# Expert stage of a two-block transformer step: inputs copied out of all assignments in expert order, nine weight slots, x summed in place, the last w2 slabs in halves

## The chip, the core and the metric

The kernel runs on one core of one Trainium2 chip. The metric is the device time of one launch in microseconds (us). The kernel is written engine by engine, with explicit semaphores: TensorE (PE) for matrix products and transposes, VectorE (DVE), ScalarE (ACT), GpSimd (POOL) and SyncE (SP). SP issues nearly all weight loads on one DMA queue; POOL issues small ones.

## The reference, cut to what matters

256 tokens of width 1024 go through a first block (attention, MLP, a state-space mixer, MLP) and a second one of two layers. Each layer of the second block is a token mixer and then a mixture of experts. Only the experts matter here:

```python
def hier_moe(h, ...):                      # h: 256 x 1024, float32
    eid, wts = ...                         # per token: top-1 group, top-2 experts of its 8; 32 experts in all
    order = argsort(eid)                   # 512 assignments (256 tokens x 2) in expert order
    for each block of assignments of one expert e:
        xb = h[tok_b]
        hid = silu(xb @ w1[e]) * (xb @ w3[e])      # w1, w3: 1024 x 512
        out[tok_b] += (hid @ w2[e]) * w_b          # w2: 512 x 1024
x = x + gate2 * out
```

Every expert's weights are read once per layer: 32 x 3 slabs of 2 MB, 96 slabs or 201 MB per layer.

## The kernel before, in words

The stages run one after the other: in, attn, mlp0, ssm, mlp1, mix0, moe0, mix1, moe1, end. `mix_*` and `moe_*` are the programs of one engine for a layer `l` (`moe_pe`, `moe_act`, `moe_dve`, `moe_pool`, `moe_sp`). Each engine waits on the semaphores of the events that it needs (`at(...)`), and each engine's program is a fixed order written out by hand.

**Pairs.** The expert stage works through `NP` = 16 pairs of experts. Each expert has room for `CAP` = 64 tokens, so a pair fills 128 columns. A flag sends the whole layer to a general path (`general_*`) when an expert has more than 64 tokens. For pair i PE does, in this order:

- `inner(i, "exp_w1")`: 16 products of 64 columns of weights against 512 columns, two experts side by side in the array; the same for `"exp_w3"`. The input is `xg`, the pair's tokens turned to columns.
- `combine(i - 1)`: four products of 128 x 512 that spread the pair before back over the 256 tokens.
- `turn_h(i)`: four transposes of the hidden rows. It waits for DVE's product `x_h`.
- `gather(i + 1)`: 16 products of 128 x 128 of the rows `H2` with a 0/1 matrix `psel` picks the next pair's tokens. ACT then scales them into `xg` (`turned_x`).
- `turn_w(i + 1)`: two transposes of the routing weights.
- `outer(i)`: 16 products with w2. It waits for ACT's copy of the turned hidden rows.

DVE makes `psel` (`places`), the weighted matrix (`weigh`), the product, the gate (`rows_out`) and the sums into `av` (`combine`).

**Weight slots.** `Places` hands out slots of 2 MB in turn. `load` takes the next slot, waits until its last tenant is free (`("free", key)`, given by PE when it has read the slab) and issues the DMA. SP does this strictly in program order: w1, w3, w2 of both experts of pair 0, then pair 1 and so on. I number the slabs 0 to 95: slabs 6i to 6i+5 belong to pair i. In the expert stage eight slots turn: four of the ring, two in the arena (`("extra", l)`, free when the mixer's branch products have been read), XTGB (free after the router) and `slot7` at the arena's end (also after `("extra", l)`). Slab n waits for slab n-8 to be read. The two slabs of the mixer's `out_w` take ring slots just before.

**Ahead of and behind the stage.** In `mix_sp` the last loads are three `branch_w` slabs and two `out_w` slabs. `moe_pool` loads the next layer's gate rows (`gate_rows`, 512 KB) and `gate_b` at the stage's start, or the final gain in layer 1. After the last pair of layer 0 a norm of x is formed, its transpose is made, and mix1 starts. After layer 1 the final norm is stored.

Of the kernel before, what the change touches and what calls it, by code (L numbers as in the profile page):

```python
# [12 lines left out]
P = 128  # L13
T = 256
# [163 lines left out]
def build(nc, d, out, consts):  # L178
    with ExitStack() as ctx:
# [15 lines left out]
        LATE = ("cm", "dmask", "rope2c", "rope2s")  # L195
        for name, width in consts.items():
            if name not in LATE:
                C[name] = sb("c_" + name, [P, width])[:, :]
        ASZ = 27124
        arena = Arena(sb("arena", [P, ASZ])[:, :], ASZ)  # L200
        posi = sb("posi", [P, 2], I32)[:, :]
        flag = sb("flag", [P, 2], I32)[:, :]
        modc = [sb(f"modc{l}", [P, 512])[:, :] for l in range(2)]
# [3 lines left out]
        for name in ("x0", "x1", "aq0", "aq1", "aq2", "aq3", "ident", "rope", "consts", "c", "pos", "gb", "sink", "ssmp", "late", "ada_b", "cols", "mod", "gate_b",  # L207
                     "fox_fb", "mla_g", "abias", "router_b", "rw", "srow", "se0", "se1", "se2", "out"):
            sems[name] = ctx.enter_context(nc.semaphore("s_" + name))
        for i in range(NRING + 4):  # L210
# [13 lines left out]
        ring = Places(slots + [None, None, XTGB, None])  # L224
# [10 lines left out]
        def slab(sp, key, name, off, kc, n, hold=False):  # L235
            load(sp, key, d[name][off:off + P * kc * n].rearrange("(p f) -> p f", p=P), kc, n, hold)

# [184 lines left out]
        def in_pool(pool):  # L422
# [3 lines left out]
            for name in consts:  # L426
                if name not in ("half", "ones", "ident", "ropec", "ropes") + LATE:
# [3 lines left out]
            pool.then_inc(pool.e.memset(C["ones"], 1.0), "ones")  # L431
# [444 lines left out]
        h00 = arena.get(2, 512)  # L876

# [16 lines left out]
        def gate_rows(pool, l, i, *events):  # L894

            pool.wait_ge(at("mod", l), *events)
            pool.landed(pool.e.dma_start(MOD[:, i, :], bcast(dmod[l][2 * i:2 * i + 2, :].rearrange("a n -> (a n)")
# [59 lines left out]
        s_E = [arena.get(2, 768) for _ in range(3)]  # L957
        spare = C["maska"]
# [69 lines left out]
        def ssm_pe(pe):  # L1028
# [10 lines left out]
            def sums():  # L1039

                pe.wait_ge(at("a"), at("consts"), at("ones"))
# [58 lines left out]
            def norm_b(g):  # L1100
                ps = bank(pe, "sn", g)
                pe.wait_ge(at("ysq", g), at("ones"))
# [222 lines left out]
        arena.pos = 0  # L1325
        for name in LATE:
            C[name] = arena.get(consts[name])
        ctab, stab = C["rope2c"], C["rope2s"]
        posf = small[:, 40:42]
        MOD = arena.get(6, D)  # L1330
# [9 lines left out]
        h01 = arena.get(2, 512)  # L1340
        rs2 = small[:, 60:62]
# [41 lines left out]

        def mlp1_pool(pool):
            pool.stage("mlp1")
            pool.wait_ge(at("XT", 3, 1))
            for name in ("cm", "dmask"):
                pool.landed(pool.e.dma_start(C[name], d["const_" + name]), "late", "late")
# [120 lines left out]
        H2, av = MOD[:, 0:2, :], MOD[:, 3:5, :]  # L1509
# [11 lines left out]
        def mix_sp(sp, l):  # L1521
# [46 lines left out]
        def causal_act(act, l, br, h, what, bufs):  # L1568
# [16 lines left out]
            elif h % 2 == 0:  # L1585
                act.wait_ge(at("cv", *k, h))
                act.then_inc(act.cp(yT[br][:, h, :], ps_of("cv", *k, h)[:, 0:T]), ("yT", l, br), ("read", "cv", *k, h))

        def causal_dve(v, l, br, h, what, bufs):
# [22 lines left out]
            elif h % 2 == 1:  # L1612
                v.wait_ge(at("cv", *k_, h))
                v.then_inc(v.cp(yT[br][:, h, :], ps_of("cv", *k_, h)[:, 0:T]), ("yT", l, br), ("read", "cv", *k_, h))
# [274 lines left out]
        def mix_dve(v, l, nn):  # L1889
# [26 lines left out]
            v.wait_ge(at("late"))  # L1916
# [40 lines left out]
            v.wait_ge(lfk, at("ones"))  # L1957
# [97 lines left out]
            for t in range(2):  # L2055
                for n in range(2):
# [3 lines left out]
                    k = v.then_inc(v.tt(o, ps_of("ob", l, t, n), MOD[:, 2, n * 512:(n + 1) * 512], ALU.mult),  # L2060
                                   ("read", "ob", l, t, n))
                    v.wait_ge(k)
                    v.then_inc(v.tt(X[:, t, hs], (av if l else X)[:, t, hs], o, ALU.add), ("rows", nn + 1, t),
# [40 lines left out]
        slot7 = arena.ap[:, ASZ - SLAB:]  # L2104
        assert arena.pos <= ASZ - SLAB
# [8 lines left out]
        g_y = slots[3][:, 0:2 * D].rearrange("p (t f) -> p t f", t=2)  # L2114
# [688 lines left out]
```

## Time and profile before

| what | value |
|---|---|
| runs | 2397.36, 2399.67, 2400.62 us (median 2399.67) |
| profiled execution | 2398.69 us |
| its span, first to last instruction | 2396.8 us |
| PE busy | 2354.6 us, 98% |
| DVE, ACT, POOL busy | 36%, 18%, 3% |
| mean granted TensorE clock | 0.994 |
| chain that ended last | PE 96%, DVE 2%, DMA 1% |
| HBM traffic | 666.56 MB read, mean 279 GB/s |

The span is the hardware profiler's; the device time is 1.9 us longer. The page's 40 slices show a DMA rate of 427 to 428 GB/s in the slices of both expert stages and 90 to 310 GB/s nearly everywhere else. "Busy" of PE counts from an instruction's start to a modelled end, so that it overlaps; for durations the distance between starts or the pieces of the chain serve better.

### The profile page before, as it was taken

Reading aid. Unit: us, or ns where it says so; the run is one execution under the profiler, and the core shown is the slowest. Engines: PE = TensorE matmul, PEld = TensorE weight load, DVE = VectorE, ACT = ScalarE, POOL = GpSimd, SP = SyncE. Lnnn points to the kernel's source line nnn. Section 1 sums busy time; section 2 is a strip of 40 time slices with the busy share of each in tenths; the row PEclk is TensorE's granted clock in tenths of the full one; section 3 lists DMA queues with packets and bytes.
Section 4 is the critical chain, followed back from the end, with each engine's and each line's share of the span. In section 5 each row is a group of like instructions: output and inputs, shape, how many; then the busy total and the mean of one; then the engine's idle time right before and its main releaser. Section 6 shows DMA issues by size and latency. Waiting matters only on the chain.

```text
span 2396.8 us, 24315 instructions
## 1 busy us (share of the span) xinstructions
PE 2354.6 (98%) x10366; PEld 1398.3 (58%) x10366; DVE 873.2 (36%) x1711; ACT 426.8 (18%) x967; POOL 74.3 (3%) x129
## 2 busy tenths in 40 slices
PE   8999999999999999999899999999999999999998
PEld 5578447875586448787444444444878644444443
DVE  3455326667355334463212222122355322112112
ACT  3310003256110011220111111101122011111111
POOL 2000000010100000000000000000000000000000
PEclk9999999999999999999999999999999999999999
DMA  7367645354577743244899999994324599999996
GB/s 281 130 229 294 276 185 195 139 192 160 189 291 271 308 147 144 96 171 181 344 428 427 427 428 428 427 427 158 114 92 170 220 373 427 428 428 427 428 428 265
DMA packets 53241, 669.44 MB, mean 279 GB/s; under 512 B 7216, under 2 KB 7504, under 8 KB 13824
## 3 DMA queue, kind: packets, MB, share of 16 engines
q1 hardware_dynamic: 46512, 649.45, 66.8%
q0 software_dynamic: 6608, 18.30, 2.3%
q8 instruction: 86, 1.41, 0.2%
q14 instruction: 35, 0.29, 0.0%
HBM read 666.56 MB, written 1.16 MB: 279 GB/s over the span
## 4 chain that ended last, share of the span: by engine, by line
PE 96%; DVE 2%; DMA 1%; issue 0%; ACT 0%; POOL 0%; SPq 0%; DVEq 0%; POOLq 0%; ACTq 0%
PE ps L101 93%; DVE arena L117 1%; PE ps L298 1%; DMA arena<-ssm_rows 1%; PE ps L2294 1%; DVE arena L114 0%; PE ps L569 0%; PE ps L2276 0%; DMA X<-in_x 0%; PE ps L1559 0%; DVE arena L110 0%; PE ps L1036 0%; POOL small L117 0%; ACT arena L106 0%; DVE arena L122 0%
## 5 line engine op out<-in xcount | busy, mean ns | idle before, releaser
L101 PE MATMUL ps<-ring,arena 128*64 128x512 f32 (+1 forms) x2368 | 703.2, 594 | 0.0
L101 PE MATMUL ps<-arena 128*128 128x128 f32 (+7 forms) x3088 | 671.5, 438 | 5.6 <-DVE arena L117 3.7
L101 PE MATMUL ps<-XTGB,ring 128*128 128x256 f32 x2800 | 618.6, 380 | 0.0
L101 PEld LDWEIGHTS ps<-XTGB,ring 128*128 128x128 f32 x2800 | 527.6, 190 | 78.7 <-issue 5.9
L101 PEld LDWEIGHTS ps<-ring,arena 128*64 128x64 f32 (+1 forms) x2368 | 264.2, 156 | 401.0 <-issue 400.1
L101 PEld LDWEIGHTS ps<-arena 128*128 128x128 f32 (+2 forms) x3088 | 337.5, 167 | 206.6 <-issue 188.9
L117 DVE TENSOR_TENSOR arena<-arena,ps 128x512 f32<-128x512 f32 x152 | 104.4, 687 | 412.3 <-PE ps L101 412.3
L101 PE MATMUL ps<-ring,XTGB 128*128 128x512 f32 (+3 forms) x568 | 226.8, 557 | 0.6 <-ACT XTGB L105 0.6
L117 DVE TENSOR_TENSOR arena<-ps,arena 128x512 f32<-128x512 f32 (+3 forms) x144 | 86.3, 634 | 318.9 <-PE ps L101 318.6
L101 PEld LDWEIGHTS ps<-ring,XTGB 128*128 128x128 f32 x568 | 106.1, 192 | 113.4 <-issue 108.0
L101 PE MATMUL ps<-XTGB,arena 128*64 128x512 f32 x384 | 169.1, 593 | 1.4 <-ACT arena L121 1.4
L121 ACT COPY arena<-ps 128x512 f32<-128x512 f32 (+2 forms) x166 | 74.1, 467 | 505.1 <-PE ps L2294 327.6
L105 ACT ACTIVATE arena<-ps 128x512 f32<-128x512 f32 x80 | 47.2, 597 | 651.7 <-PE ps L101 651.7
L117 DVE TENSOR_TENSOR arena<-arena 128x256 f32<-128x256 f32 (+8 forms) x220 | 109.1, 508 | 113.4 <-ACT arena L105 108.8
L114 DVE SCALAR_TENSOR_TENSOR arena<-ring,small,arena 128x512 f32<-128x512 f32 x168 | 126.3, 752 | 6.0
L122 DVE COPY arena<-ps 128x256 f32<-128x256 f32 (+3 forms) x64 | 29.7, 469 | 240.3 <-PE ps L2276 118.0
L101 PEld LDWEIGHTS ps<-XTGB,arena 128*64 128x64 f32 x384 | 51.9, 137 | 107.2 <-issue 105.4
L105 ACT ACTIVATE arena<-ps,small 128x128 f32<-128x128 f32 (+1 forms) x264 | 100.0, 457 | 66.9 <-PE ps L101 66.8
L114 DVE SCALAR_TENSOR_TENSOR arena<-arena 128x256 f32<-128x256 f32 (+1 forms) x212 | 87.8, 438 | 52.2 <-ACT arena L105 29.1
L128 DVE RECIPROCAL arena<-arena 128x2 f32<-128x2 f32 (+2 forms) x84 | 90.0, 1071 | 3.8 <-ACT arena L106 1.8
L101 PE MATMUL ps<-arena,ring 128*128 128x256 f32 x384 | 83.2, 379 | 0.0
L101 PEld LDWEIGHTS ps<-arena,ring 128*128 128x128 f32 x384 | 72.8, 190 | 9.8
(155 smaller groups left out, 781.6 us busy)
## 6 DMA issues: line engine op xcount, KB each, us to landing
ring<-in_exp_w SPq DMA_DIRECT2D x96, 2048.0 KB, 18.8
arena<-in_exp_w SPq DMA_DIRECT2D x72, 2048.0 KB, 20.1
ring<-in_mlp_w SPq DMA_DIRECT2D x32, 2048.0 KB, 7.8
ring<-in_ada_w SPq DMA_DIRECT2D x24, 2048.0 KB, 8.2
XTGB<-in_exp_w SPq DMA_DIRECT2D x24, 2048.0 KB, 17.3
ring<-in_ssm_w_in SPq DMA_DIRECT2D x12, 2048.0 KB, 7.8
ring<-in_w_in SPq DMA_DIRECT2D x12, 2048.0 KB, 7.9
ring<-in_gate_w SPq DMA_DIRECT2D x12, 2048.0 KB, 7.9
```

Source lines behind the costliest of these rows:

```text
L101: return self.e.matmul(o, lhsT=lhsT, rhs=rhs, start=start, stop=stop, skip_group_check=True)
L105: return self.e.activation(o, i, func, bias=bias, scale=scale)
L114: return self.e.scalar_tensor_tensor(out=o, in0=i0, scalar=s, in1=i1, op0=op0, op1=op1)
L117: return self.e.tensor_tensor(o, a, b, op)
L121: return self.e.copy(o, i)
L122: return self.e.tensor_copy(o, i)
L128: return self.e.reciprocal(o, i)
L298: ins = pe.e.transpose(ps[:, j * P:(j + 1) * P], i, C["ident"][0:m, 0:m])
L2294: ins = pe.e.transpose(ps[:, f * P:(f + 1) * P], x_h[:, f:512:4], C["ident"])
```

## The change

- **Order.** `order()` on DVE, run in pair 0, forms the start of each expert in the list of all 512 assignments by five doubling sums (`cnt`), writes the starts as integers (`wsi`, at most `LAST` = 448), corrects `code` for late experts, and builds `selc`, a 256 x 512 matrix of 0 and 1 that puts each assignment into its place.
- **Compaction.** PE's `compact(c)` multiplies each of the eight chunks of `H2` by `selc`: two products of 128 x 512 per chunk. Four chunks go behind `combine(0)` in pair 1, four behind `combine(1)` in pair 2. ACT scales them into `compA` and `compB`. `compA` lies over the tables `cm` and `dmask`, which are loaded again at the end of layer 0 (`late_tables`).
- **From the fourth pair on** (`ND` = 3) PE's `gather` is left out. ACT's `window(i)` reads two starts into registers and copies four blocks of 4 x 64 columns out of the compacted rows.
- **Order on PE.** `combine` is cut in halves: one ahead of `turn_h`, one behind it. In pair 0 the halves of `gather(1)` stand there.
- **Nine slots.** Two slots at the arena's end, 7 and 8, are free when the mixer's attention is done; the two `out_w` slabs take them. Slab n then waits for slab n-9.
- **x in place.** The experts' sums go into `X`. A copy of `X` (1 MB) is written to DRAM at the stage's start, for the general path. Gate rows and final gain are loaded after the last compaction.
- **Last w2.** In pair 15 the two w2 slabs are loaded as four half slabs (first output half of both, then the second half).
- `ones` becomes a view of `tri`; `maska`, `ropec`, `ropes` and `modc` move into the arena.

```diff
+        def slabs_in_halves(sp, keys, name, offs, kc, n):
+            place = {}
+            for h in range(2):
+                for j, (key, off) in enumerate(zip(keys, offs)):
+                    if h == 0:
+                        place[key], was = ring.take(key)
+                        if was is not None:
+                            sp.wait_ge(at("free", was))
...
+                    sp.landed(sp.e.dma_start(o, src), f"half{j}" if h else f"ring{place[key]}", ("w half" if h else "w", key))
# mix_sp
+            for j in (4, 3):
+                ring.tenant[NRING + j] = ("attention", l)
+            ring.turn[0:0] = [NRING + 4, NRING + 3]
# moe_pool
-            pool.wait_ge(at("rows", nn - 1, 1))
+            pool.wait_ge(at("rows", nn - 1, 0), at("rows", nn - 1, 1))
+            pool.landed(pool.e.dma_start(dkeep[l], X), "keep", ("keep", l))
+            pool.landed(pool.e.dma_start(iota, d["const_iota512"]), "iota", ("iota", l))
             if l == 0:
-                gate_rows(pool, 1, 2)
                 pool.landed(pool.e.dma_start(gb, d["gate_b"][P:2 * P, :]), "gate_b", ("gate_b", 1))
+                gate_rows(pool, 1, 2, at("comp", l, 7))
+                pool.wait_ge(at("xg ready", l, NP - 1, 0), at("xg ready", l, NP - 1, 4))
+                late_tables(pool, 1)
# moe_pe
+            def compact(c):
+                ps = bank(pe, "comp", l, c)
+                pe.wait_ge(at("selc", l))
+                for t in range(2):
+                    ins = pe.mm(ps, H2[:, t, c * P:(c + 1) * P], selc[:, t, :], t == 0, t == 1)
+                pe.then_inc(ins, ("comp", l, c))
...
                 inner(i, "exp_w3")
                 if i >= 1:
-                    combine(i - 1)
+                    combine(i - 1, 0)
+                else:
+                    gather(1, 0)
                 turn_h(i)
+                if i >= 1:
+                    combine(i - 1, 1)
+                else:
+                    gather(1, 4)
+                for c in COMPACT.get(i, ()):          # {1: (0, 1, 2, 3), 2: (4, 6, 5, 7)}
+                    compact(c)
+                if 1 <= i < ND - 1:
+                    gather(i + 1, 0)
+                    gather(i + 1, 4)
                 if i + 1 < NP:
-                    gather(i + 1)
                     turn_w(i + 1)
                 outer(i)
# moe_act
+            def window(i):
+                act.wait_ge(at("comp ready", l), at("starts", l), at("exp_w3", l, i - 1))
+                first = [start_of(act, 2 * i + j) for j in range(2)]
+                for c0, comp in ((0, compA), (4, compB)):
+                    for j in range(2):
+                        act.then_inc(act.cp(xg[:, c0:c0 + 4, 64 * j:64 * j + 64], comp[:, :, bass.ds(first[j], CAP)]),
+                                     ("xg ready", l, i, c0))
```

## Rows read from the trace of the kernel before

**Rows 1.** The page: busy time, share and instructions of each engine.
```profile
PE 2354.6 (98%) x10366; PEld 1398.3 (58%) x10366; DVE 873.2 (36%) x1711; ACT 426.8 (18%) x967; POOL 74.3 (3%) x129
```

**Rows 2.** Windows: stretch, length, busy by engine, clock, DMA share, GB/s.
```profile
1560.00:1590.00 30.00, 30.00 (x150) 13.04 (x148) 5.25 (x9) 4.19 (x10) 0.00 (x0) 1.00 1.01 428
```

**Rows 3.** The chain in moe0: start, length, what; one pair.
```profile
1206.68 3.57 PE ps L101 x32
...
1210.47 24.38 PE ps L101 x104
...
1239.11 24.38 PE ps L101 x104
```

**Rows 4.** Tile view, time to landing of the last slab, issued at 1575.35.
```profile
DMA to landing us min/median/max: 31.7/31.7/31.7
```

**Rows 5.** The chain around the last pair of moe0.
```profile
1607.21 0.48 PE ps L2294 x4
...
1608.40 9.87 PE ps L101 x38
```

**Rows 6.** Timeline of SP: the issues of weight slabs (x2: two slabs).
```profile
1149.84 0.33 SPq L233 DMA_DIRECT2D XTGB<-in_exp_w  x1
...
1169.08 0.80 SPq L233 DMA_DIRECT2D ring<-in_exp_w  x2
...
1188.88 0.81 SPq L233 DMA_DIRECT2D ring<-in_exp_w  x2
...
1202.62 0.80 SPq L233 DMA_DIRECT2D ring<-in_exp_w  x2
1217.53 0.80 SPq L233 DMA_DIRECT2D arena<-in_exp_w  x2
...
1246.17 0.92 SPq L233 DMA_DIRECT2D ring<-in_exp_w  x2
```

**Rows 7.** Tile view, time to landing of slab 8, issued at 1169.08.
```profile
DMA to landing us min/median/max: 7.8/7.8/7.8
```

**Rows 8.** Tile view, time to landing of slab 12, issued at 1188.88.
```profile
DMA to landing us min/median/max: 9.4/9.4/9.4
```

**Rows 9.** Tile view, time to landing of slab 17, issued at 1202.99.
```profile
DMA to landing us min/median/max: 19.8/19.8/19.8
```

**Rows 10.** Timeline of PE in pair 0 of moe0: `turn_h(0)`.
```profile
1177.28 0.75 PE L2294 MATMUL ps<-c_ident,arena 128*128 128x128 f32 x4 [0.86 <-DVE arena L117]
```

**Rows 11.** Timeline of PE: `combine(14)`, four products of 128 x 512 (two passes each).
```profile
1603.51 3.70 PE L101 MATMUL ps<-arena 128*128 128x512 f32 x8
```

**Rows 12.** DMA view: issues, KB each, median us to landing.
```profile
arena<-mod POOLq DMA_DIRECT2D x4, 512.0 KB, 12.5
...
arena<-in_const_dmask POOLq DMA_DIRECT2D x1, 768.0 KB, 11.1
...
arena<-in_const_cm POOLq DMA_DIRECT2D x1, 192.0 KB, 6.1
```

**Rows 13.** Tile view, time to landing of slab 93 in moe0, issued at 1568.49.
```profile
DMA to landing us min/median/max: 27.5/27.5/27.5
```

**Rows 14.** Tile view, time to landing of slab 93 in moe1, issued at 2336.39.
```profile
DMA to landing us min/median/max: 27.7/27.7/27.7
```

**Rows 15.** The chain at the last `outer` of moe1.
```profile
2376.31 9.87 PE ps L101 x38
```

**Rows 16.** Windows: an idle stretch of PE, the stretch behind, and a short gap.
```profile
1618.70:1622.60 3.90, 0.42 (x1) 0.00 (x0) 1.92 (x4) 2.71 (x4) 0.56 (x1) 1.00 0.93 384
...
1624.20:1627.80 3.60, 3.48 (x4) 1.45 (x5) 2.38 (x6) 0.68 (x2) 2.05 (x2) 0.53 0.08 32
...
573.00:576.00 3.00, 2.33 (x20) 1.38 (x19) 2.90 (x7) 0.19 (x1) 0.63 (x1) 1.00 0.00 0
```

**Rows 17.** Timeline of ACT in moe0, last pair.
```profile
1607.72 0.58 ACT L121 COPY arena<-ps 128x512 f32<-128x512 f32 x1 [10.36 <-PE ps L2294]
```

**Rows 18.** Source view: ACT loads a register.
```profile
L2209 ACTq TENSOR_LOAD <-flag x1: 479/479/479, 1210.3 to 1210.3; - x1
```

More of the change, by code:

```diff
@@ L220, in build @@
                 sems[f"gen{l}_w{j}"] = ctx.enter_context(nc.semaphore(f"s_gen{l}_w{j}"))
-        ring = Places(slots + [None, None, XTGB, None])
+            sems[f"gen{l}_x"] = ctx.enter_context(nc.semaphore(f"s_gen{l}_x"))
+        ring = Places(slots + [None, None, XTGB, arena.ap[:, ASZ - 2 * SLAB:ASZ - SLAB], arena.ap[:, ASZ - SLAB:]])
         ring.begin(NRING)
@@ L1382, in mlp1_sp, with late_tables @@
             mlp_sp(sp, 1)
+        def late_tables(pool, l):
+            for name in ("cm", "dmask"):
+                pool.landed(pool.e.dma_start(C[name], d["const_" + name]), "late", ("late", l))
         def mlp1_pool(pool):
@@ L1386, in mlp1_pool @@
             pool.wait_ge(at("XT", 3, 1))
-            for name in ("cm", "dmask"):
-                pool.landed(pool.e.dma_start(C[name], d["const_" + name]), "late", "late")
+            late_tables(pool, 0)
             for i in (2, 5):
@@ L1586, in causal_act @@
                 act.wait_ge(at("cv", *k, h))
-                act.then_inc(act.cp(yT[br][:, h, :], ps_of("cv", *k, h)[:, 0:T]), ("yT", l, br), ("read", "cv", *k, h))
+                act.then_inc(act.cp(yT[br][:, h, :], ps_of("cv", *k, h)[:, 0:T]), ("yT", l, br), ("read", "cv", *k, h),
+                                *([("free", ("attention", l))] if br == 2 else []))
         def causal_dve(v, l, br, h, what, bufs):
@@ L1613, in causal_dve @@
                 v.wait_ge(at("cv", *k_, h))
-                v.then_inc(v.cp(yT[br][:, h, :], ps_of("cv", *k_, h)[:, 0:T]), ("yT", l, br), ("read", "cv", *k_, h))
+                v.then_inc(v.cp(yT[br][:, h, :], ps_of("cv", *k_, h)[:, 0:T]), ("yT", l, br), ("read", "cv", *k_, h),
+                              *([("free", ("attention", l))] if br == 2 else []))
         def mix_pe(pe, l, nn):
@@ L2113, in build @@
         g_u = x_h.rearrange("p (a b) -> p a b", a=2)
-        g_y = slots[3][:, 0:2 * D].rearrange("p (t f) -> p t f", t=2)
+        g_y, g_x = [slots[3][:, 2 * D * i:2 * D * (i + 1)].rearrange("p (t f) -> p t f", t=2) for i in range(2)]
+        g_a = arena.ap[:, xbase:xbase + 2 * D].rearrange("p (t f) -> p t f", t=2)
+        dkeep = [nc.dram_tensor(f"x{l}", (T, D), F32).ap().rearrange("(t p) f -> p t f", t=2) for l in range(2)]
         g_h = xg.rearrange("p a b -> p (a b)").rearrange("p (a b) -> p a b", a=4)
@@ L2235, in moe_sp @@
                         slab(sp, (nm, l, i, j), nm, (l * NE + 2 * i + j) * P * SLAB, 8, 512)
-                for j in range(2):
-                    slab(sp, ("exp_w2", l, i, j), "exp_w2", (l * NE + 2 * i + j) * P * SLAB, 4, 1024)
+                keys = [("exp_w2", l, i, j) for j in range(2)]
+                offs = [(l * NE + 2 * i + j) * P * SLAB for j in range(2)]
+                if i < NP - 1:
+                    for key, off in zip(keys, offs):
+                        slab(sp, key, "exp_w2", off, 4, 1024)
+                else:
+                    slabs_in_halves(sp, keys, "exp_w2", offs, 4, 1024)
             general(sp, l, reg, general_sp)
@@ L2317, in outer, with combine @@
                         pe.then_inc(ins, ("xy", l, i, n), *([("free", ("exp_w2", l, i, j)) for j in range(2)] if n else []))
[L2319 to L2328 removed]
+            def combine(i, n):
+                pe.wait_ge(at("pwt ready", l, i), at("xy ready", l, i, n))
+                for t in range(2):
+                    ps = bank(pe, "xc", l, i, t, n)
+                    pe.then_inc(pe.mm(ps, pwt[i % 2][:, t * P:(t + 1) * P], x_y[:, n * 512:(n + 1) * 512],
+                                      True, True), ("xc", l, i, t, n))
+            for c0 in (0, 4):
+                gather(0, c0)
             for t in range(2):
@@ L2378, in moe_act @@
                              ("xht ready", l, i), ("read", "xht", l, i))
-                if i + 1 < NP:
+                for c in COMPACT.get(i, ()):
+                    compact(c)
+                if i + 1 < ND:
                     turned_x(i + 1)
+                elif i + 1 < NP:
+                    window(i + 1)
                 if i == 1:
@@ L2529, in moe_dve @@
                     weigh(i + 2)
+                if i == 0:
+                    order()
             rows_out(NP - 1)
@@ L2669, in constants @@
     c["ident"] = np.eye(P, dtype=f)
-    c["ones"] = None
     c["half"] = None
```

188 lines of the change are left out of this document (125 added, 63 removed).

## Prediction, made before the change was run

> **What bounds the kernel now.** I read the page first. PE is busy 98% of the span [rows 1], so a change that takes matrix products away looks like a gain. The windows show that this is only half of it: in the expert stages the DMA engines are full as well, 428 GB/s with a share of 1.01 [rows 2]. So I compare the two by pair. On the chain of moe0 the starts of the same piece lie 1239.11 - 1210.47 = 28.64 us apart [rows 3]; that is PE's time for a pair. The six slabs of a pair cost the DMA: slab 8 lands at 1169.08 + 7.8 = 1176.9, slab 12 at 1188.88 + 9.4 = 1198.3, slab 17 at 1202.99 + 19.8 = 1222.8 [rows 6 to 9]. The last five take 24.5 us, 4.90 each, which agrees with 2.097 MB at 428 GB/s; six take 29.4 us. **DMA is therefore slower than PE by 0.7 us a pair**, and PE hides it only with the lead that it gets from slabs loaded during the mixer. At the end that lead is gone: the last slab lands at 1575.35 + 31.7 = 1607.05 [rows 4], and the `outer` that reads it starts at 1608.40 [rows 5]. Taking work off PE can't shorten a stage whose transfers end 1.3 us before they are needed. Only an earlier or fuller DMA queue can, or a shorter chain behind the last slabs.
>
> When does the queue stand idle? Slab 8 is issued at 1169.08 when `inner(0, "exp_w1")` frees its slot, after slab 7 has long landed. Between slabs 8 and 12 lie 21.4 us, 1.9 more than four transfers: slab 12 was issued at 1188.88, when `outer(0)` freed its slot, and the queue ran dry at 1176.9 + 3 x 4.9 = 1191.6 (slab 11), only 2.7 us later. From issue to first byte it takes 7.8 - 4.9 = 2.9 us with an empty queue, and 9.4 - 4.9 = 4.5 us here [rows 7, 8]. Slab 18, issued at 1217.53 [rows 6], was 5.3 us ahead of slab 17's landing and lost nothing, by the full windows behind it.
>
> **The change part by part.** Everything is counted in moe0; moe1 repeats it.
>
> *PE's units.* A piece of 24.38 us holds 48 products that run two by two and 4 full ones, 28 units of 0.87 us [rows 3]; the four of `combine` alone read 3.70 us [rows 11], so 0.87 to 0.93. An `inner` or `outer` is 8 units, 6.97 us, half a `combine` 1.74.
>
> *Gathers gone.* 3.57 us each [rows 3], 13 of 16: -46.4 us of PE a layer. *Compaction:* eight chunks of two full products, 16 x 0.87 = +13.9 us, 6.97 in each of pairs 1 and 2. From pair 3 on a pair takes 28.64 - 3.57 = 25.07 us. Net -32.5 us of PE, nearly all of it worth nothing, because the DMA's 29.4 us a pair are then late.
>
> *Ninth slot.* Nine slabs instead of eight are in before PE frees the first slot at 1169.08: the slab for the slot behind the mixer's first `out_w` (about 1137), its second, and the one into XTGB at 1149.84 [rows 6]. The DMA is idle before 1169.08, so the ninth is free: **-4.9 us** on everything behind.
>
> *Pair 0.* PE waits 0.86 us for DVE ahead of `turn_h(0)` [rows 10]; half a gather now covers that. `outer(0)` frees its slots 0.86 us earlier, 3.5 us before the queue is dry: idle at most 1.0 instead of 1.9. **-0.9 us**.
>
> *Pair 1, a new idle.* Slab 19 (slab 18 takes the place that slab 17 had, and lands at 1222.8 - 0.9 = 1221.9) needs slab 10's slot, freed by `outer(1)`. That end moves from 1217.53 to 1217.53 - 0.86 + 6.97 = 1223.6, with the queue already empty. First byte at +2.9 = 1226.5: **+4.6 us**.
>
> *Pair 2, again.* Slab 24 ends at 1226.5 + 6 x 4.9 = 1255.9. Slab 25 needs `outer(2)`, at 1246.17 - 0.86 + 13.94 - 3.57 = 1255.7 [rows 3, 6]. First byte 2.9 to 4.5 us later, 1258.6 to 1260.2: **+2.7 to +4.3 us**. The gate rows of 512 KB (1.2 us at 428 GB/s) [rows 12], now issued after the last compaction, fall into this gap and cost nothing more. From pair 3 on PE frees slots 4.3 us a pair faster than they fill, so no further idle.
>
> Sum for the DMA: -4.9 - 0.9 + 4.6 + (2.7 to 4.3) = **+1.5 to +3.1 us**: the four edits that should feed the queue are more than eaten by the compaction, which holds back two releases at the worst moment.
>
> *Reloaded tables,* moe0 only: 768 + 192 KB [rows 12] issued when `xg` of pair 15 is ready, into a full queue ahead of slab 93: 0.98 MB / 428 GB/s = **+2.3 us**. I count them fully, since windows at 1.01 leave no room beside them; below, 0. The copy of X (1 MB), the 512-wide counts and `gate_b` run in the idle stretch that ends at 1169.08: some 3 us beside one slab issued at 1149.84, 0 (if late, at most 2).
>
> *Behind the last slabs.* PE catches the DMA up: slab 19 lands at 1231.4 and pair 3 starts near 1256, a lead of 24.5 us that shrinks by 4.3 a pair, so from pair 9 on PE waits for w1 and w3 of every pair. In the last pair slab 93 decides. Before it lands at 1568.49 + 27.5 = 1596.0 [rows 13] and `outer(15)` starts 12.4 us later. After: 0.2 for the semaphore, `inner` 6.97, half a combine 1.74 (covers DVE's product), `turn_h` 0.48 [rows 5], the other half 1.74 (covers ACT's copy of 0.58 [rows 17]) = 11.1 us. The w2 slabs need 9.8 us, so they are in; **halves gain nothing** (if their smaller rows slowed them by up to a third, the second half would still come before 11.1 + 3.5 us).
>
> moe0: 1596.0 + (1.5 to 3.1) + 2.3 + 11.1 = 1610.9 to 1612.5 against 1608.40 [rows 5]: **+2.5 to +4.1 us**. moe1: slab 93 lands at 2336.39 + 27.7 = 2364.1 [rows 14]; + (1.5 to 3.1) + 11.1 = 2376.7 to 2378.3 against 2376.31 [rows 15]: **+0.4 to +2.0 us**. Behind `outer(15)` both orders are the same.
>
> *Clock.* New idle gaps of PE appear from pair 9 on: 2.7 us ahead of w3 (9.8 - 6.97) and about 1.5 ahead of w1. The rows show the granted clock at 0.53, the level of 1.2 GHz, for 3.6 us behind an idle stretch of nearly 3.9 us, and still 1.00 where PE was busy 2.33 of 3.00 us [rows 16]. My gaps lie between the two. A fall costs half of 3.6, 1.7 us, and inside the stage the waits absorb it; it counts only in the last `inner` or `outer`: 0 to 1.7 us a layer. I take 0.6 each, 1.2 in all.
>
> On such gaps the Trainium skill ("TensorE: Matmul & The Clock Gate", section "HAM oscillation") is blunter: it describes a kernel whose bursts are shorter than its waits for weights and which is throttled anew at each of them. By that rule every wait here would be paid with slow products; the trace of before, whose expert stages have no such gaps, can't confirm it. It is the third rival.
>
> *ACT, DVE, POOL, SP.* ACT's window is two register loads of 0.48 [rows 18] and four copies of 256 elements, at most 0.58 each [rows 17], 3.3 us after the x_ht copy; PE passes 1.74 + 0.22 + 6.97 us before it needs them. Queued behind it on ACT is only the next silu. `order()` adds some twenty DVE instructions in pair 0, where DVE is busy 5.9 of 30 us in such a window [rows 2]; only `rows_out(0)` stands behind, 14 us ahead of its reader. POOL waits with nothing behind it but the flag and the norm. SP is held up by the attention's end for the two `out_w` slabs, which are needed tens of us later. All 0; if the register loads drained ACT, up to 5 us a pair would still be covered.
>
> **Sum.** 2.5 to 4.1 + 0.4 to 2.0 = +2.9 to +6.1, middle 4.5, with the clock 5.7. The profiled execution took 2398.69 us (span 2396.8 and 1.9 around it), 1.0 below the median of 2399.67: 2398.7 + 5.7 = 2404.4, or 2405.4 from the median. **I predict 2405 us.**
>
> **Rivals.**
>
> 1. *The queue is never dry (faster).* The place is slabs 19 and 25. If `outer(1)` and `outer(2)` freed their slots 4.5 us before the queue ends, the -5.8 us would stand: moe0 1596.0 - 5.8 + 2.3 + 11.1 = 1603.6 (-4.8), moe1 2364.1 - 5.8 + 11.1 = 2369.4 (-6.9): 2387. It decides once PE's compaction costs under about 1.5 us a pair, or the lead is larger than I count. Against it: 0.87 us a product is read off. 12%.
> 2. *No change.* The idle at slab 25 vanishes because PE is a little faster than counted and slab 24 slower; that takes 2.7 to 4.3 off each layer: -2 us in all, 2397. 20%.
> 3. *The clock (slower still).* All three waits of a pair, from pair 9 on, end in a fall: 25.07 + 3 x 1.7 = 30.2 us, 0.8 above the DMA's 29.4, over seven pairs and two layers 11 us: 2398.7 + 4.5 + 11 = 2415. 11%.
> 4. *The windows are late.* PE waits for ACT in each of 13 pairs; 1 us beyond the covered stretch would cost 13 a layer less the slack of 4.3 a pair. 5%, near 2410.
>
> **How the numbers follow.** My forecast (2401 to 2409 with its clock) has 52%. Within 0.2%, 4.8 us, is about what a measurement can't tell from no change. Of the forecast 60% lies above +4.8: 0.31, with rivals 3 and 4 0.47 slower. Same: 0.21 and most of rival 2, 0.36. Faster: rival 1 and a rest of 2, 0.17. The range leaves out rival 1's core and the far end of 3: 2391 to 2413.
>
> **What would show it.** Landing times: slab 18 near 1222, slab 19 near 1231.4, slab 25 near 1264 (1261.9 before); SP's issue of slabs 19 and 25 with an empty queue; windows below 400 GB/s near 1224 and 1257; PE's chain in the last pairs waiting on the DMA with 29.4 us a pair; slab 93 of moe0 near 1601, of moe1 near 2366; PE's busy share down by some 60 us and a clock below 0.99. If PE shows no wait on weights in the late pairs, or slab 25 lands before 1259, I am wrong.

## The result, and the profile after

The changed kernel takes **2404.97 us** (median of 9 runs, 2403.39 to 2408.97) against 2399.67 us before; the ratio is 1.0026 with a 95% interval of [1.0015, 1.0036]. It is slower by some 5 us, and whether by more than 0.2% the interval leaves open. The profiled execution took 2406.85 us, 1.9 above its own median, while that of before lay 1.0 below its own; the two traces therefore differ by 8.2 us and the medians by 5.3. The section on the prediction says which terms this touches.

The page of the changed kernel, busy time and then the chain of waits by engine:

```profile
PE 2313.4 (96%) x9598; PEld 1329.6 (55%) x9598; DVE 881.3 (37%) x1751; ACT 395.2 (16%) x879; POOL 77.6 (3%) x134
...
PE 83%; DMA 14%; DVE 2%; issue 0%; ACT 0%; POOL 0%; SPq 0%; DVEq 0%; POOLq 0%; ACTq 0%
```

PE does 41 us less than before [rows 1], and the kernel is longer all the same: 14% of the chain is now DMA. The time is lost in the stretches that the windows of the changed kernel show (stretch, length, busy by engine, clock, DMA share, GB/s): two in pairs 1 and 2, and three around the last `inner` of moe0:

```profile
1222.50:1227.50 5.00, 5.00 (x26) 1.63 (x24) 1.29 (x2) 0.00 (x0) 0.00 (x0) 1.00 0.32 69
1257.50:1261.50 4.00, 4.00 (x20) 1.28 (x18) 0.81 (x2) 0.00 (x0) 0.00 (x0) 1.00 0.87 310
1600.00:1602.60 2.60, 0.44 (x3) 0.00 (x0) 0.00 (x0) 0.60 (x1) 0.00 (x0) 1.00 0.97 370
1602.80:1606.40 3.60, 3.60 (x10) 1.34 (x12) 0.00 (x0) 0.00 (x0) 0.00 (x0) 0.53 1.04 385
1606.50:1610.00 3.50, 3.50 (x18) 1.38 (x16) 0.00 (x0) 0.00 (x0) 0.00 (x0) 1.00 1.05 386
```

Near 1224 the queue moves 69 GB/s while PE is fully busy: PE is still at the compaction and holds the slot that the next slab needs. Before, the expert stages run at 428 GB/s [rows 2]. The landing times of the slabs that were issued into these gaps, from the tile view (slab 19, issued at 1225.1; slab 25, at 1257.1; slab 93 of moe0, at 1568.3; slab 93 of moe1, at 2342.2; each line is one slab's time from issue to landing):

```profile
DMA to landing us min/median/max: 8.1/8.1/8.1
...
DMA to landing us min/median/max: 9.2/9.2/9.2
...
DMA to landing us min/median/max: 34.3/34.3/34.3
...
DMA to landing us min/median/max: 30.6/30.6/30.6
```

So slab 19 lands at 1233.2, slab 25 at 1266.3, and slab 93 at 1602.6 and 2372.8. A slab that took 8.1 us had an empty queue in front of it, as slab 8 had before [rows 7]. The chain of the changed kernel in moe0 (start, length, what) reads first as before, then differently:

```profile
1218.03 22.66 PE ps L101 x100
...
1249.96 22.66 PE ps L101 x100
...
1275.03 22.66 PE ps L101 x100
...
1300.11 22.66 PE ps L101 x100
...
1364.18 29.31 DMA arena<-in_exp_w
...
1393.63 10.70 PE ps L101 x36
...
1568.32 34.27 DMA ring<-in_exp_w
1602.59 0.14 issue
1602.73 10.70 PE ps L101 x36
1613.42 0.47 PE ps L2370 x4
1613.89 11.52 PE ps L101 x42
```

Without its gather a pair takes PE 1300.11 - 1275.03 = 25.08 us (before 28.64 [rows 3]). From pair 3 on PE is therefore faster than the DMA, catches it up near 1380 and then waits. The end of the stage is the landing of slab 93 plus what stands behind it; the last `outer` starts at 1613.89 + 1.72 = 1615.6 against 1608.40 [rows 5].

To compare stages I take POOL's instruction in the normalisation that ends each of them. Timeline of POOL in the changed kernel, behind moe0, behind the mixer and behind moe1 (start, length, what, idle before):

```profile
1627.59 0.56 POOL L117 TENSOR_TENSOR small<-small,c_half 128x1 f32<-128x1 f32 x1 [43.55 <-DVE small L111]
...
1923.20 0.56 POOL L117 TENSOR_TENSOR small<-small,c_half 128x1 f32<-128x1 f32 x1 [16.14 <-DVE small L111]
...
2396.10 0.56 POOL L117 TENSOR_TENSOR small<-small,c_half 128x1 f32<-128x1 f32 x1 [373.10 <-DVE small L111]
```

The same instruction stands at 1149.86 ahead of moe0. Before, the four are 1148.97, 1620.44, 1916.81 and 2388.36. As stage lengths in us, with the experiments of the next section:

```
                       moe0    mixer   moe1
before                471.5    296.4   471.6
changed               477.7    295.6   472.9
e1_double             491.5    298.5   486.9
e2_narrow             472.7    296.1   468.8
e3_eight              480.6    295.8   478.9
e5_tables_later       477.1    296.0   475.0
e6_whole_w2           474.8    297.9   474.2
e7_filler             475.9    296.1   473.3
e4_no_copying         470.4    296.2   469.4
e8_no_copying_whole   470.1    295.6   469.6
e9_no_copying_eight   469.5    296.8   470.3
e10_no_copying_uncut  472.1    296.6   471.7
```

One execution stands in each line. e6 differs from the changed kernel only where nothing waits (below), so its 2.9 us less in moe0 and 1.3 more in moe1 are roughly what one stage varies by. The changed kernel's moe0 is 6.3 us longer than before in these traces; e5, e6 and e7, which do nearly the same work, are 5.6, 3.3 and 4.4 longer, so 6.3 is the high end.

### The profile page after: what moved, and what is told of

Its sections match the earlier page's. It is cut to its first block, busy times and chain, and to the rows that moved or that the text cites. A ratio compares the mean times of both kernels' runs of the same rounds, so it can differ in the third digit from the quotient of the medians.

```text
span 2405.0 us, 23014 instructions
## 1 busy us (share of the span) xinstructions
PE 2313.4 (96%) x9598; PEld 1329.6 (55%) x9598; DVE 881.3 (37%) x1751; ACT 395.2 (16%) x879; POOL 77.6 (3%) x134
## 4 chain that ended last, share of the span: by engine, by line
PE 83%; DMA 14%; DVE 2%; issue 0%; ACT 0%; POOL 0%; SPq 0%; DVEq 0%; POOLq 0%; ACTq 0%
PE ps L101 81%; DMA ring<-in_exp_w 8%; DMA arena<-in_exp_w 5%; DVE arena L117 1%; PE ps L322 1%; DMA arena<-ssm_rows 1%; DVE arena L114 0%; PE ps L2370 0%; DMA ring<-in_attn_w_in 0%; PE ps L592 0%; PE ps L1600 0%; PE ps L2352 0%; PE ps L1061 0%; DVE arena L110 0%; ACT arena L106 0%
## 5 line engine op out<-in xcount | busy, mean ns | idle before, releaser
L101 PE MATMUL ps<-arena 128*64 128x512 f32 (+7 forms) x2640 | 697.1, 517 | 23.3 <-DMA arena<-in_exp_w 17.7
L101 PEld LDWEIGHTS ps<-arena 128*64 128x64 f32 (+2 forms) x2640 | 290.2, 160 | 333.6 <-issue 309.9
L117 DVE TENSOR_TENSOR arena<-ps,arena 128x512 f32<-128x512 f32 (+4 forms) x166 | 96.0, 613 | 358.1 <-PE ps L101 345.1
L117 DVE TENSOR_TENSOR arena<-arena,ps 128x512 f32<-128x512 f32 x32 | 22.0, 688 | 463.8 <-PE ps L101 463.8
L101 PE MATMUL ps<-XTGB,arena 128*64 128x512 f32 x320 | 148.9, 620 | 12.0 <-DMA ring<-in_exp_w 11.9
L121 ACT COPY arena<-ps 128x512 f32<-128x512 f32 (+3 forms) x167 | 74.6, 467 | 518.2 <-PE ps L2370 338.9
L105 ACT ACTIVATE arena<-ps 128x512 f32<-128x512 f32 (+1 forms) x81 | 47.6, 594 | 677.9 <-PE ps L101 677.8
L114 DVE SCALAR_TENSOR_TENSOR arena<-arena 128x256 f32<-128x256 f32 (+2 forms) x216 | 90.8, 444 | 51.1 <-ACT arena L105 28.6
L117 DVE TENSOR_TENSOR X<-X,ps 128x512 f32<-128x512 f32 x128 | 88.1, 688 | 40.0 <-PE ps L101 40.0
L122 DVE COPY arena<-ps 128x256 f32<-128x256 f32 (+5 forms) x67 | 30.2, 455 | 183.3 <-PE ps L101 121.3
```

Of the source, the lines that this page charges most:

```text
L101: return self.e.matmul(o, lhsT=lhsT, rhs=rhs, start=start, stop=stop, skip_group_check=True)
L105: return self.e.activation(o, i, func, bias=bias, scale=scale)
L114: return self.e.scalar_tensor_tensor(out=o, in0=i0, scalar=s, in1=i1, op0=op0, op1=op1)
L117: return self.e.tensor_tensor(o, a, b, op)
L121: return self.e.copy(o, i)
L122: return self.e.tensor_copy(o, i)
```

## The experiments

My theory was that the compaction in pairs 1 and 2 holds back two slot releases, that the DMA queue runs dry there, and that every microsecond of this reaches the end because the stage is bound by transfers. The rivals: the waits of PE in the late pairs (its clock), the reloaded tables, the windows on ACT, and that the gain of the gathers was only hidden by something small at the end. e1 to e3 price the theory, e4 takes its cause away, e5 to e7 test the rivals, and e8 to e10 ask what in the change is worth keeping.

**e1_double: the compaction at twice its price.**

```diff
-                for t in range(2):
+                for t in (0, 1, 0, 1):
                     ins = pe.mm(ps, H2[:, t, c * P:(c + 1) * P], selc[:, t, :], t == 0, t == 1)
```

> The changed kernel with each compaction product run twice, the second pass over the first, so that the values stay the same; PE gets 16 more products of 0.87 us a layer, 6.9 us in each of pairs 1 and 2. My theory: in these pairs PE decides when slots come free, so the DMA stands idle for just that time: slab 19 starts 6.9 us later, slab 25 another 6.9 us minus what it now overlaps, some 12 us a layer, 25 in all: 2430 us. Rival (PE has slack in a stage that waits for weights, compaction is free): 2405. Rival (the clock and the additional small transfers made the loss): 2405 too.

2436.74 us (5 runs, 2436.39 to 2436.83), ratio 1.0156 [1.0142, 1.0170]: 31.8 us above the changed kernel. Windows of e1 where slabs 19 and 25 are due, and POOL's instruction behind moe0 and moe1:

```profile
1222.00:1234.00 12.00, 12.00 (x66) 5.33 (x67) 2.47 (x5) 3.02 (x8) 0.00 (x0) 1.00 0.15 38
1258.00:1272.00 14.00, 14.00 (x56) 5.16 (x56) 2.47 (x5) 2.78 (x6) 0.54 (x1) 1.00 0.50 184
```

```profile
1640.72 0.56 POOL L117 TENSOR_TENSOR small<-small,c_half 128x1 f32<-128x1 f32 x1 [41.54 <-DVE small L111]
...
2426.07 0.56 POOL L117 TENSOR_TENSOR small<-small,c_half 128x1 f32<-128x1 f32 x1 [373.17 <-DVE small L111]
```

The queue stands idle for 11.3 us ahead of slab 19 and 8.4 ahead of slab 25, where the changed kernel had 5.1 and 2.9. The stages grow by 13.8 and 14.0 us, and the added products are 13.9 us a layer: **close to one for one**. Counted from POOL's instruction ahead of the stage, slab 25 lands 12.1 us later than in the changed kernel in moe0 and 13.3 in moe1, about the 12 that I had expected; the rest comes behind it and is within what a stage varies by. The mixer adds 2.9, all of it between POOL's first and second instruction behind moe0 (7.9 against 4.9 us); I can't explain it. All of this work was given to the engine that waits for weights from pair 7 on: that it costs nearly its full length shows that the bound isn't PE's total but when PE frees slots.

**e2_narrow: the compaction at a quarter of the columns.**

```diff
-                    ins = pe.mm(ps, H2[:, t, c * P:(c + 1) * P], selc[:, t, :], t == 0, t == 1)
+                    ins = pe.mm(ps[:, 0:P], H2[:, t, c * P:(c + 1) * P], selc[:, t, 0:P], t == 0, t == 1)
```

> The changed kernel with each compaction product 128 columns wide instead of 512; the copied inputs of the assignments beyond the first 128 are wrong. PE loses 10.4 us of work a layer in pairs 1 and 2, nothing else changes: nine slots, all transfers, the copies, the late gaps stay. My theory: the idle stretch of the DMA ahead of slab 19 shrinks from 4.6 to about 1 us and the one ahead of slab 25 vanishes, 6 us a layer, 12 in all: 2393 us, below the kernel before. Rival (compaction is hidden, the loss lies in the clock, the small transfers or the half slabs): 2405, no change.

2396.58 us (11 runs), ratio 0.9989 [0.9980, 0.9998]: 8.4 us below the changed kernel. Windows of e2 at the same places:

```profile
1222.00:1227.00 5.00, 5.00 (x26) 1.68 (x24) 0.00 (x0) 0.60 (x1) 0.00 (x0) 1.00 1.00 419
1257.00:1260.00 3.00, 3.00 (x13) 0.95 (x10) 0.69 (x1) 0.00 (x0) 0.00 (x0) 1.00 1.01 431
```

The gaps are gone (0.8 us ahead of slab 19, none ahead of slab 25), slab 93 of moe0 lands at 1595.7. Of the 6 us a layer that I expected 5.0 and 4.1 came. The timeline of PE shows where the rest of moe0 went:

```profile
1595.82 9.62 PE L101 MATMUL ps<-ring,arena 128*64 128x512 f32 x32 [4.29 <-DMA ring<-in_exp_w]
```

PE was further ahead, waited 4.29 us and ran the last `inner` in 9.62 instead of 7 us. Even with a nearly free compaction this kernel is only 2.4 us faster than before, and e4 below, which saves no gather at all, is as fast or faster (2394.97), while e2 still reloads the tables (2.4 us, see e5). So the gathers saved, 46 us of PE a layer, show no gain of their own.

**e3_eight: the change with eight slots.**

```diff
-            for j in (4, 3):
+            for j in (3,):
-ring.turn[0:0] = [NRING + 4, NRING + 3]
+ring.turn[0:0] = [NRING + 3]
```

> The changed kernel with eight weight slots: the ninth, slot 8, is left out and the second out_w slab goes into a ring slot again. My theory: one transfer of 4.9 us a layer moves behind PE's first release and the dry stretches grow by about 1 us: 6 us a layer, 12 in all: 2417 us. Rival (the slot count doesn't matter once PE waits for weights): 2405. Rival (the ninth slot costs, by an earlier collision in the mixer): below 2405.

2417.70 us (5 runs, 2414.94 to 2419.49), ratio 1.0080 [1.0066, 1.0093]. By the medians the ninth slot is worth 12.7 us here, 6.4 a layer. By the landing of slab 93, counted from POOL's instruction ahead of each stage, it is 4.6 us in moe0 and 4.5 in moe1, close to the 4.9 of one transfer; what the rest of the 12.7 is, I can't say from one trace each (the profiled execution of e3 was the fastest of its five). The window of e3 in pair 1 shows the same gap, one slab earlier in number (it is slab 18 now that waits 5.0 us):

```profile
1217.00:1228.00 11.00, 11.00 (x54) 3.66 (x52) 2.02 (x4) 0.84 (x3) 0.00 (x0) 1.00 0.61 225
```

**e4_no_copying: every pair gathers again,** the rest of the change stays (nine slots, x summed in place, halves, the cut `combine`).

```diff
-        ND = 3
+        ND = NE // 2
-COMPACT = {1: (0, 1, 2, 3), 2: (4, 6, 5, 7)}
+COMPACT = {}
```

(and `order()`, the wide counts, the reloaded tables and the waits for `comp` go, so that the gate rows and the final gain are loaded at the stage's start again.)

> The changed kernel without its copied inputs: every pair's tokens are gathered by PE as before, and order(), the compaction, the 512-wide counts, the windows and the reload of the tables are gone; nine slots, the cut combine, x in place and the half slabs stay. My theory: PE again needs 28.6 us a pair and decides the end, the DMA is 5.8 us a layer ahead of it; what is left of the change is 0.86 us in pair 0 and about 0.9 behind the last slab: 1 to 2.5 us a layer faster than the kernel before, 2395 to 2398. Rival (the copying is what helps and another part costs): above 2405. Rival (nine slots alone bring their 4.9 us a layer): 2388.

2394.97 us (11 runs), ratio 0.9986 [0.9977, 0.9995]: **10.0 us faster than the changed kernel, although PE does 41 us more.** Slab 93 lands at 1590.8 and 2356.4, counted from POOL's instruction ahead of the stage 4.4 and 5.7 us earlier than before, and PE no longer waits for weights. This is what the other edits give together; the copying took it and more.

**e5_tables_later: the reload of the tables behind the last pair.**

```diff
-                pool.wait_ge(at("xg ready", l, NP - 1, 0), at("xg ready", l, NP - 1, 4))
+                pool.wait_ge(at("xy", l, NP - 1, 1))
                 late_tables(pool, 1)
```

> The changed kernel with the reload of cm and dmask at the end of moe0 issued when outer(15) has run, behind all weight slabs, instead of when the input of pair 15 is ready. My theory: 0.98 MB leave the full queue ahead of slab 93, which lands 2.3 us earlier in moe0; moe1 has no reload: 2402.7 us, ratio to before 1.0015. Rival (the small transfers share the engines without cost): 2405, ratio 1.0025. Rival (the tables are now late for mix1): above 2405.

2404.51 us (11 runs), ratio 1.0023 [1.0014, 1.0032], no difference to the changed kernel. Counted from POOL's instruction ahead of moe0, slab 93 lands 2.5 us earlier (1599.2 - 1149.0 against 1602.6 - 1149.9), about the 2.3 that I had put down, though 1.1 of them are there at slab 25 already, ahead of any reload. The reload itself is read best from slab 87 to slab 93, six transfers: 32.1 us in moe0 of the changed kernel, 29.4 in moe0 of e5 and 29.4 in moe1 of both. It costs the queue 2.7 us; in moe0 of e1, e2, e3, e6 and e7, which all reload, it is 2.4 to 2.6. But the stage is only 0.6 us shorter. First the timeline of POOL in e5, then the chain:

```profile
1619.28 0.54 POOL L1417 DMA_DIRECT2D arena<-in_const_cm  x1 [369.02 <-PE ps L101]
1619.81 0.54 POOL L1417 DMA_DIRECT2D arena<-in_const_dmask  x1
```

```profile
1610.22 11.52 PE ps L101 x42
...
1623.67 0.17 DVE small L111
1623.84 2.27 issue
1626.11 0.57 POOL small L117
```

The two issues went onto POOL right ahead of the normalisation's own POOL instruction, which was ready at 1623.84 and started 2.27 us later (0.07 in the changed kernel). In this trace the move exchanged one cost for another.

**e6_whole_w2: the last w2 slabs whole.**

```diff
-                if i < NP - 1:
+                if True:
                     for key, off in zip(keys, offs):
```

> The changed kernel with the last two w2 slabs whole instead of in halves. My theory: outer(15) starts 11.1 us or more behind slab 93, and the w2 slabs need 9.8 whole and 10.8 in halves, so both are in: 0, 2405 us, at most 1 us less because the next stage's loads stand behind 1 us less of transfers. Rival (the halves let outer(15) start early): whole slabs cost up to 2 us a layer, 2409. Rival (the smaller rows hold the queue back and cost): 2403 or less.

2406.20 us (7 runs), ratio 1.0029 [1.0018, 1.0041]: no difference. With slab 93 at 1600.1 the last slab lands at 1609.9, and `outer` can't start before some 11 us after slab 93. In the changed kernel the last half lands at 1613.4 and `outer` starts at 1615.6, so the halves were not waited for either.

**e7_filler: PE kept busy through its waits** from pair 9 on, by products whose result nobody reads.

```diff
+                if i >= 9:
+                    for _ in range(3 if nm == "exp_w3" else 1):
+                        pe.mm(ps, C["ident"], C["tri"], True, True)
                 pe.wait_ge(at("w", (nm, l, i, 0)), at("w", (nm, l, i, 1)))
```

> The changed kernel with filler products in PE's waits: from pair 9 on one product of 128 x 512 of constants ahead of inner w1 and three ahead of inner w3, into the bank that the inner then overwrites; 3.5 us a pair, less than the 4.3 us of slack. My theory: the granted clock of the span goes from 0.986 back to 0.99 or more and the last inner w3 of moe0 takes 7.1 instead of 8.8 us; that is worth 0 to 1.7 us a layer, for only the last inner counts: 2403 to 2405. Rival (the slow clock is the main loss): 2400 or less. Rival (PE has no slack there): 2410 or more.

2404.81 us (11 runs), ratio 1.0024 [1.0015, 1.0033]: no difference that the interval can tell; the granted clock of the span went from 0.986 to 0.992. The timeline of PE in e7 from the filler ahead of the last `inner` of moe0 to that `inner`, then of the changed kernel at the last two `inner` of moe0 and the last one of moe1:

```profile
1597.98 2.84 PE L101 MATMUL ps<-c_tri,c_ident 128*128 128x512 f32 x6
...
1602.44 7.09 PE L101 MATMUL ps<-ring,arena 128*64 128x512 f32 x32 [1.61 <-DMA ring<-in_exp_w]
```

```profile
1591.66 8.78 PE L101 MATMUL ps<-ring,arena 128*64 128x512 f32 x32 [2.57 <-DMA ring<-in_exp_w]
...
1602.73 8.78 PE L101 MATMUL ps<-ring,arena 128*64 128x512 f32 x32 [2.29 <-DMA ring<-in_exp_w]
...
2372.93 7.09 PE L101 MATMUL ps<-ring,arena 128*64 128x512 f32 x32 [2.67 <-DMA ring<-in_exp_w]
```

The filler saves 1.7 us in that one `inner`, and moe0 is 1.8 shorter; moe1, whose last `inner` ran at full clock anyway, is 0.4 longer. So the clock is here a term of at most one such fall a layer; the stage lengths alone, which vary by more, would not show it.

**e8_no_copying_whole, e9_no_copying_eight, e10_no_copying_uncut: what is left.** e8 is e4 with whole w2 slabs; e9 is e8 with eight slots (the edit of e3); e10 is e8 with `combine` whole in every pair and the first gather whole in pair 0, in the order of the kernel before:

```diff
                 if i >= 1:
                     combine(i - 1, 0)
-                else:
-                    gather(1, 0)
+                    combine(i - 1, 1)
                 turn_h(i)
-                if i >= 1:
-                    combine(i - 1, 1)
-                else:
-                    gather(1, 4)
+                if i == 0:
+                    gather(1, 0)
+                    gather(1, 4)
```

> The version that the first four runs point to: nine slots, cut combine, x in place, every pair gathered, no compaction, windows or reload, and the last w2 slabs whole. My theory: PE decides the end and the last slabs come over 3 us before they are needed, so whole or half makes no difference: 2394 to 2396, 4 us below the kernel before. Rival (the halves carry part of the 4 us): 2397 or more.

> The version without copied inputs and with whole w2 slabs, but with eight weight slots instead of nine. My theory: the DMA's last slabs then land 4.9 us later, about 1596 in moe0, which is just where PE wants them; the ninth slot is worth only what PE had to wait, 0 to 2.5 us a layer: 2395 to 2399, against 2394.7 with nine. Rival (the slot is what made that version faster than the kernel before): 2399 or more, all of the 4 us gone. Rival (slots don't matter when PE decides): 2394.7.

> The same version with nine slots, but combine and the gather of pair 0 whole: all of combine(i-1) ahead of turn_h(i), nothing behind it, as in the kernel before. Nine slots and x in place stay. My theory: the 0.86 us in pair 0 and the 0.7 us ahead of outer(15) come back, 1.6 us a layer: 2397.5 to 2398.5. Rival (the nine slots carry the gain): 2394.7.

e8: 2394.69 us, ratio 0.9983 [0.9974, 0.9992], the fastest version of this study. e9: 2396.64 us, 0.9987 [0.9978, 0.9996]. e10: 2398.84 us, 0.9999 [0.9990, 1.0008] (11 runs each). So nearly the whole gain against before, 4.4 us, goes when `combine` and the first gather are no longer cut around `turn_h` (e10; the two intervals just touch, the medians lie 4.2 us apart), and the ninth slot adds 2 us or nothing (e9, intervals overlap). The cut pays at two places of a layer only. In e10 the two waits of PE that it had filled are back; timeline of PE at `turn_h(0)` and at the last `outer` of moe0:

```profile
1177.87 0.75 PE L2366 MATMUL ps<-c_ident,arena 128*128 128x128 f32 x4 [0.86 <-DVE arena L117]
...
1608.99 1.51 PE L101 MATMUL ps<-arena 128*64 128x512 f32 x6 [0.72 <-ACT arena L121]
```

Slab 24 is issued 1.2 us later in moe0 than in e8 and 1.4 in moe1, counted from POOL's instruction ahead of the stage; up to slab 92 nothing is added, and the stages end 2.0 and 2.2 later. I had forecast 0.86 and 0.7. Nine slots and x in place alone (e10 against before) gave nothing that the interval can tell. The chain of e8 at the end of moe0:

```profile
1582.27 22.66 PE ps L101 x100
1604.93 0.47 PE ps L2366 x4
1605.40 11.52 PE ps L101 x42
```

It is all PE: the last `outer` starts inside the piece at 1605.40, half a `combine` in, near 1607.1, while its slabs are there since 1601.3. With the queue never dry behind slab 9 the DMA is off the path, and PE's own waits are worth taking out; the cut fills them.

## Why the prediction came out right, step by step

The time (2405.0 against 2404.97) and the mechanism held. That it came so close is luck: the nine runs spread over 5.6 us, and some of the terms were off, partly against each other.

*Bound.* That taking products off PE is worth nothing was right, and e4 and e8 show it from the other side: with the gathers put back and the compaction gone the kernel is 10 us faster.

*Ninth slot and pair 0.* Slab 18 was forecast at 1221.9 and landed at 1223.2. Of the 1.3 us, 0.9 were there at POOL's instruction ahead of moe0 (1149.86 against 1148.97), where nothing is changed; the ten experiments lie between 1148.2 and 1149.7 there, so this is one execution's offset. Without it slab 18 lands 0.5 us earlier than slab 17 did before (1.0 in moe1), forecast 0.9. The price of the slot was 4.9 in my sum; taken away (e3) it costs 4.6 and 4.5 by the landing of slab 93 and 6.4 a layer by the medians, and in a kernel that PE bounds (e9 against e8) at most 1. A slot has no price of its own.

*The idle at slab 19:* 5.1 us in moe0 and 4.8 in moe1, forecast 4.6. *At slab 25:* 2.9 in moe0 and 1.1 in moe1, forecast 2.7 to 4.3. "Near 1264" became 1266.3: slab 25 was issued at 1257.0 instead of 1255.7 (0.9 of it the offset) and took 4.3 us to its first byte, the upper part of what I had put down. Slab 24 holds something that I had not counted: it lands 5.7 us behind slab 23 in moe0 and 6.6 in moe1 instead of 4.9. The gate rows (issued at 1250.5, landed at 1259.8) and in moe1 the final gain (2022.5 to 2032.1) are in flight there, and in moe0 of e8, which loads the gate rows at the stage's start, slab 24 takes 4.9; in e2, which issues the gate rows at 1238.9, it is slab 23 that takes 6.2. So they fall ahead of the gap at least in part, and not into it as I had written, at 0.8 and 1.7 us; in moe1 the idle at slab 25 is shorter for it. The idle stretches are the step on which the sign hung, and e1 and e2 show that they come from the compaction: twice its price gives 11.3 and 8.4, a quarter 0.8 and nothing. That nearly each microsecond of it then goes through to the end was implied in my sum but not said; e1 measured it.

*Reloaded tables.* 2.7 us by the six transfers up to slab 93 (32.1 against 29.4), forecast 2.3. I had not forecast that moving them would gain nothing (e5).

*DMA sum.* Slab 93 of moe0 lands 6.6 us later than before, 5.7 without the offset, from POOL's instruction on; forecast 3.8 to 5.4 with the tables. The measured terms, -4.9 - 0.5 + 5.1 + 0.8 + 2.9 + 2.7, come to 6.1. In moe1 it lands at 2372.8, not "near 2366": I had written down an absolute time without adding what moe0 hands on. From POOL's instruction ahead of each moe1 it is 2372.8 - 1923.2 = 449.6 against 2364.1 - 1916.8 = 447.3, +2.3, forecast +1.5 to +3.1; the measured terms there, -4.9 - 1.0 + 4.8 + 1.7 + 1.1, come to 1.7.

*Behind slab 93.* Forecast 11.1 us to `outer`; moe0 took 13.0 (1602.6 to 1615.6) and moe1 11.3. The difference of 1.7 is the fallen clock in the last `inner`, 8.78 against 7.09 us. I had priced it at 0 to 1.7 and taken 0.6 for each layer; in this trace it was the upper end once and the lower end once, 1.7 instead of 1.2 in all.

*PE's waits and busy time.* I placed the first wait in pair 9. It came in pair 7 (0.3 us) and is 1.2 us or more from pair 8 on. The lead shrinks by 29.4 - 25.08 = 4.3 us a pair as I said, but I had counted it at slab 19, ahead of the second gap. The 3.7 us of slabs 24 and 25 come off it: (24.5 - 3.7) / 4.3 = 4.8 pairs behind pair 3, which is pair 7 to 8. The waits for weights on PE in both expert stages (waits of the changed kernel from 1150 to 2400: us in total, times, longest):

```profile
PE ps L101 <- DMA ring<-in_exp_w: 32.5, 13, 3.4
PE ps L101 <- DMA arena<-in_exp_w: 20.2, 11, 2.6
```

PE's busy time fell by 41 us, not by some 60. The products removed and added come to 65 by the prices of [rows 3]; most of the other 24 us are products that ran slowly: the mean clock of the span fell from 0.994 to 0.986, which is by estimate 19 us of 2,400 (the clock over 1300 to 1500 reads 0.98 with PE busy 187.4 of 200 us). I had priced a fall and not carried it into this forecast; the last 5 us stay open. The mean clock of the span, 0.986, is below 0.99 as said.

*Halves.* Nothing, as forecast (e6).

*Slips in the working.* The window of [rows 2] shows DVE busy for 5.25 of 30 us, not 5.9, and the sum of the third rival is 2414, not 2415. Neither bears on the forecast.

*Rivals.* "The queue is never dry" did not happen in the change, and e2 and e4 come nearest to it: 2396.6 and 2395.0, not 2387. In e4 PE takes over as the bound, which my 2387 left out. In e2 the transfers stay the bound (the wait of 4.29 us above), but slab 93 lands at 1595.7 and not at the 1596.0 - 5.8 + 2.3 = 1592.5 of this rival, and the last `inner` takes 9.62 us; 0.8 of the 3.2 us are the idle left at slab 19, the others I haven't placed. "No change" fell: slab 25 landed at 1266.3. "The windows are late" fell: the timeline of ACT in the changed kernel in an early pair

```profile
1273.13 0.59 ACT L121 COPY arena<-ps 128x512 f32<-128x512 f32 x1 [8.64 <-PE ps L2370]
...
1274.30 1.33 ACT L121 COPY arena<-arena 128x256 f32 x4 [0.58 <-issue]
```

shows them done 2.5 us after the start of the copy ahead of them, and PE never waits for them. "The clock at every wait" was wrong in its sum: PE is on the path only behind the last slab. In this trace a wait doesn't always end in a fall either: in pair 9 an `inner` of 32 products behind 2.39 us of idle (start 1423.00) took 7.09 us, and the last one of moe1 behind 2.67 us as well. The Trainium skill ("TensorE: Matmul & The Clock Gate", section "HAM oscillation — how this bites in real kernels") describes a fall at each wait for weights, in a kernel whose bursts of products are shorter than its waits. By that rule, so I wrote, every wait here would be paid with slow products. That took the page too far, for here the bursts are 7 us and more and the waits 1.2 to 3.4. The trace shows a fall at some of the waits, and e7 shows that the total hardly depends on it here.

Where the time comes from, then: my two traces differ by 0.9 ahead of moe0, 6.3 in it, -0.8 in the mixer and 1.3 in moe1. Of moe0's 6.3, 5.7 lie ahead of slab 93's landing (queue and tables) and 0.5 behind it, where one slow `inner` of 1.7 eats what the shorter order gains; of moe1's 1.3, 2.3 lie ahead of it and -1.0 behind. The medians differ by 5.3, so some 3 us of the traces' 8.2 are the variation of single executions, and I claim no finer split.

## What to carry to other kernels

When two engines are nearly equal over a stage, the one that frees the buffers decides when the other may start. Here 13.9 us a layer added to PE while the queue was nearly empty came back almost in full at the end, and 46 us taken off it gave nothing. A change that bundles several edits wants its cheap ones run alone: here the cut of `combine` and of the first gather around one wait was worth some 4 us, 2 a layer, in a kernel that PE bounds, and the large edit took it back.

## What the hardware showed that I had not expected

- **The clock fell after short waits.** The granted clock reads 0.53, the level of 1.2 GHz, over 3.6 us (1602.80 to 1606.40) behind 2.29 us of idle; PE was busy without a break for 7 us or more between such gaps. I had seen it before only behind 3.9 us [rows 16]. Behind 2.39 us in pair 9 and 2.67 us at the end of moe1 it did not fall; the length of the gap alone doesn't decide. In moe0 of the changed kernel there are twelve waits of 1.2 us or more, and six such stretches of slow clock.
- **Half slabs are slower than their bytes, and hold their issuer.** The tile view of the changed kernel for the halves of moe0 (duration of the issue in ns min/median/max, first and last start):

```profile
L260 SPq DMA_DIRECT2D arena<-in_exp_w x4: 652/1938/19777, 1568.7 to 1599.0; - x4
```

  They land at 1605.3, 1608.0, 1610.7 and 1613.4, 2.70 us for 1 MB against 2.45 for half of a whole slab's 4.90, 10% more. One issue took 19.8 us on SP; issues of whole slabs take 0.3 to 0.4. Here the fourth half stood behind it and still landed 2.7 us behind the third, so nothing was lost; that another transfer issued from SP would have been late by it is argued, not shown.
- **A DMA issue on POOL costs more than its 0.54 us.** Two of them ended at 1620.35 and the next POOL instruction, ready at 1623.84, started at 1626.11 (e5), though 3.5 us had passed; in the changed kernel, where the two issues came 44 us earlier, it started 0.07 us after it was ready. What POOL did in between the trace doesn't show.
